# Input and output stored by feature, the first norm applied to projection results, and a different attention tail

## The reference

```
h = rms_norm(x, norm_pre[layer])                 # over the 2048 features of a token
qkv_a, z_a, b_a, g_a, q_b, k_b, v_b, z_b = split(h @ w_in)
qkv_a = silu(causal_depthwise_conv(qkv_a, conv_w))       # 4 taps along the tokens
y_a = rms_norm(gated_delta_rule(...), a_norm) * silu(z_a)
p = softmax(q k^T masked by chunks of 64)
o_b = (p[0] - lam * p[1]) @ v                     # per head, 512 x 128
y_b = rms_norm(o_b, b_norm) * (1 - lam_init) * silu(z_b)
x = x + rms_norm(concat(y_a, y_b) @ w_out, norm_post[layer])
```

## Time and profile before

| | us |
|---|---|
| median of 3 runs | 2717.47 (2712.59 to 2721.62) |
| the profiled execution, its own time | 2727.59 |
| its span, first to last instruction | 2725.3 |
| PE busy | 2550.4 (94% of the span) |
| DVE busy | 1260.8 (46%) |
| ACT busy | 843.0 (31%) |
| POOL busy | 282.2 (10%) |

### The profile page before, as it was taken

How to read it: one execution, slowest core, us unless ns; L and a number is a source line. 1 busy time by engine, 2 the same in 40 slices (tenths; PEclk the granted TensorE clock), 3 DMA queues, 4 the chain that set the end, 5 groups by cost and what they waited for, 6 DMA issues and landing times.

```text
span 2725.3 us, 31273 instructions
## 1 busy us (share of the span) xinstructions
PE 2550.4 (94%) x12516; PEld 2114.8 (78%) x12516; DVE 1260.8 (46%) x1642; ACT 843.0 (31%) x1320; POOL 282.2 (10%) x190
## 2 busy tenths in 40 slices
PE   5999999999999998899978979999999999998897
PEld 4788787888877777888866758888888888887666
DVE  4554545554454447562255455334433344334644
ACT  4232323232244344442232341222212222223333
POOL 0010010202100100001140150000000000013104
PEclk9999999999999999999989989999999999998898
DMA  8932322165344331452212212333333332222211
GB/s 183 106 71 52 63 49 69 39 63 56 70 113 80 75 84 64 130 177 96 100 55 70 70 51 89 96 97 95 97 93 91 100 100 92 101 93 70 70 62 70
DMA packets 221721, 231.84 MB, mean 85 GB/s; under 512 B 9392, under 2 KB 214448, under 8 KB 220848
## 3 DMA queue, kind: packets, MB, share of 16 engines
q1 hardware_dynamic: 221472, 229.83, 33.8%
q10 hardware_dynamic: 144, 0.52, 0.1%
HBM read 221.94 MB, written 8.39 MB: 85 GB/s over the span
## 4 chain that ended last, share of the span: by engine, by line
PE 62%; issue 22%; DVE 7%; POOL 5%; ACT 3%; DMA 1%; DVEq 0%; SPq 0%; POOLq 0%; ACTq 0%
PE acc L757 19%; PE acc L759 18%; PE acc L758 18%; POOL residual L1731 3%; POOL work L1684 2%; DVE weights_lo L1107 1%; ACT weights_hi L365 1%; PE m L912 1%; PE m L1010 1%; PE m L736 1%; DVE work L1505 1%; ACT work L675 1%; PE m L920 1%; DMA work<-in_lambda 1%; PE m L1036 1%
## 5 line engine op out<-in xcount | busy, mean ns | idle before, releaser
L757 PE MATMUL acc<-input_hi,weights_hi 128*128 128x512 f32 (+1 forms) x3200 | 1268.8, 397 | 75.6 <-DVE input_lo L1499 42.4
L759 PE MATMUL acc<-input_hi,weights_lo 128*128 128x512 f32 (+1 forms) x3200 | 1234.8, 386 | 0.0
L758 PE MATMUL acc<-input_lo,weights_hi 128*128 128x512 f32 (+1 forms) x3200 | 1234.4, 386 | 0.0
L1107 DVE TENSOR_TENSOR weights_lo<-weights_raw,weights_hi 128x1024 fp32r<-128x1024 f32 x400 | 497.2, 1243 | 962.1 <-ACT weights_hi L365 961.6
L757 PEld LDWEIGHTS acc<-input_hi,weights_hi 128*128 128x128 f32 x3200 | 613.0, 192 | 216.4 <-issue 67.0
L365 ACT ACTIVATE weights_hi<-weights_raw 128x1024 fp32r<-128x1024 f32 x400 | 423.2, 1058 | 1026.9 <-PE acc L759 1004.9
L759 PEld LDWEIGHTS acc<-input_hi,weights_lo 128*128 128x128 f32 x3200 | 611.4, 191 | 121.8
L758 PEld LDWEIGHTS acc<-input_lo,weights_hi 128*128 128x128 f32 x3200 | 613.2, 192 | 111.2 <-issue 1.9
L1723 POOL TENSOR_TENSOR work<-work 128x512 f32<-128x512 f32 x56 | 72.3, 1291 | 1145.5 <-ACT work L629 1141.1
L1667 POOL TENSOR_TENSOR small<-small 128x4 f32<-128x4 f32 (+1 forms) x20 | 25.8, 1289 | 817.2 <-DVE small L1295 429.7
L1731 POOL TENSOR_TENSOR residual<-residual,work 128x512 f32<-128x512 f32 x59 | 93.0, 1609 | 43.7 <-DVE work L1505 43.7
(11 more groups left out here) (235 smaller groups left out, 1812.6 us busy)
## 6 DMA issues: line engine op xcount, KB each, us to landing
weights_raw<-in_ab_w_in SPq DMA_DIRECT2D x128, 512.0 KB, 5.2
weights_raw<-in_c_w_in SPq DMA_DIRECT2D x128, 512.0 KB, 3.7
weights_raw<-in_m_w_kv SPq DMA_DIRECT2D x32, 512.0 KB, 3.4
weights_raw<-in_ab_w_out SPq DMA_DIRECT2D x32, 512.0 KB, 3.2
weights_raw<-in_m_w_q SPq DMA_DIRECT2D x32, 512.0 KB, 3.3
weights_raw<-in_c_w_out SPq DMA_DIRECT2D x32, 512.0 KB, 3.2
weights_raw<-in_m_w_o SPq DMA_DIRECT2D x16, 512.0 KB, 3.2
work<-in_x SPq DMA_DIRECT2D x4, 1024.0 KB, 10.8
```

The lines of the kernel that those rows point to most:

```text
L757: pe.matmul(out, w_hi[:, o:o + P], hi(kt), start=kt == 0, stop=False)
L758: pe.matmul(out, w_hi[:, o:o + P], lo(kt), start=False, stop=False)
L759: last = pe.matmul(out, w_lo[:, o:o + P], hi(kt), start=False, stop=kt == last_kt)
L1107: TTO(w_lo[:, s * CW:(s + 1) * CW], raw[:, c * CW:(c + 1) * CW], w_hi[:, s * CW:(s + 1) * CW].bitcast(F32), ALU.subtract).then_inc(lo_read ...
```

## The change

Five edits. (1) The host passes x transposed, [16, 128, 512], so `residual` is loaded directly; ACT makes the high part of x times gain, DVE the low part (a scalar_tensor_tensor), and the spill buffer goes: the read-back takes x again. (2) The inverse root mean square is left out of the projection's input and applied when layer 0's projections are evacuated (`take_z`, `convolve`, `keep`, the gate columns). Squares of x are made by ACT, summed by POOL over the 16 tiles, by PE over partitions. (3) The first two column groups, z and q, alternate: chunk order z0 q0 z1 q1 and so on for 8 chunks, with x tiles between the loads; the gate columns move behind chunk 7. (4) Attention's last product swaps its operands, so the output stands by token; ACT's square gives each token's sum at once; DVE scales, PE turns the tile by 4 transposes (hop `ft`), and the hops get weights of their own. (5) The output is stored by feature straight from `residual`, and one more of the last adds goes to DVE.

```diff
@@ hops
-    B_HOPS += ["fs" + _h, "fb" + _h]
+    B_HOPS += ["ft" + _h]
-VECTOR_ADDS = (1, 4, 7, 10, 13)
+B_REPLY = {"vt": 1.2, "a": 0.8, "a00": 2.0, "a10": 2.0, "b": 1.2, "b03": 1.8, "b13": 1.8, "f": 0.6}
+D_SLOTS, B_SLOTS = weighted(D_HOPS, 12, 63, D_REPLY), weighted(B_HOPS, 18, 63, B_REPLY)
+VECTOR_ADDS = (1, 4, 7, 10, 13, 15)
+START_SPLITS = {(0, 0): 0, (0, 1): 1, (1, 1): 2, (1, 3): 3, (2, 1): 4, (2, 3): 5, (3, 1): 6, (3, 3): 7}
+def start_chunk(c):
+    return (c % 2, 4 * (c // 2)) if c < 8 else (c // 4, 4 * (c % 4))
@@ ACT, start
-            for k in range(KT):
-                act.wait_ge(*SM(f"tr{k}"))
-                act.activation(xt(k), start_banks[k % 4], ACT.Copy).then_inc(*SA.did(f"copy{k}"))
-                if k:
-                    start_high(k - 1)
+            def start_high(k):
+                act.wait_ge(x_in[k], 16)
+                act.activation(H_hi[:, k * T:(k + 1) * T], xt(k), ACT.Copy, scale=pcol("norm_pre", k))\
+                    .then_inc(*SA.did(f"hi{k}"))
+            for q in range(4):
+                for n in range(4):
+                    start_high(4 * q + n)
+                    if (q, n) in START_SPLITS:
+                        split(C_AB + START_SPLITS[q, n])
+                for n in range(4):
+                    start_square(4 * q + n)
@@ PE, gates (now at c == 8)
+                        if k == 2:
+                            pe.wait_ge(*SG("sum"))
+                            for t in range(TT):
+                                last = pe.matmul(M[0][:, t:t + 1], sq_sum[:, t * P:(t + 1) * P], ones, ...)
+                        if k == 14:
+                            pe.wait_ge(*SG("pow"))
+                            rows(lambda t: M[2][:, t * P:(t + 1) * P], lambda t: powed[:, t:t + 1], TT)
@@ attention tail: ACT, PE, DVE
-                    act.activation(o_sb, M[3], ACT.Copy).then_inc(*BA.did())
-                    act.activation(o_sq, M[3], ACT.Square).then_inc(*BA.did(f"o{name[1]}"))
+                    for t in range(TT):
+                        act.activation(o_sq[:, o], M[3][:, o], ACT.Square, accum_out=stat[:, t:t + 1])
-                        last = pe.matmul(M[0][:, t:t + 1], o_sq[:, t * P:(t + 1) * P], ones, start=True, stop=True)
-                else:
-                    last = rows(lambda t: M[0][:, t * P:(t + 1) * P], lambda t: powed[:, t:t + 1], TT)
+                else:
+                    pe.wait_ge(*BV("on" + name[2], i))
+                    for t in range(TT):
+                        last = pe.transpose(M[0][:, t * P:(t + 1) * P], o_sb[:, t * P:(t + 1) * P], ident)
+                elif name in ("b03", "b13"):
+                    dve.wait_ge(*BA("o" + h, i))
+                    TS(stat[:, 0:4], stat[:, 0:4], 1.0 / HD, EPS, ALU.mult, ALU.add).then_inc(*BV.did("stat" + h))
+                    dve.wait_ge(*BG("pow" + h, i))
+                    TTO(tiles(o_sb), tiles(M[3]), over_row(powed[:, 0:4], TT, P), ALU.mult).then_inc(*BV.did("on" + h))
-                    then(STT(out=o_sb, in0=o_sb, scalar=b_gain, in1=M[0], op0=ALU.mult, op1=ALU.mult))
-                    TTO(y, y, o_sb, ALU.mult).then_inc(*BV.did(f"y{h}"))
+                    STT(out=y, in0=M[0], scalar=b_gain, in1=y, op0=ALU.mult, op1=ALU.mult).then_inc(*BV.did(f"y{h}"))
@@ DVE, evacuation of layer 0
+                TTO(conv_in, bank(1 + sec, n), rs[:, :], ALU.mult).then_inc(acc_free, 1)
-                TS(dst, src, tap(3), None, ALU.mult).then_inc(*EV.did())
+                TS(dst, conv_in, tap(3), None, ALU.mult).then_inc(*EV.did())
-                dve.tensor_copy((qc, kc, vc)[sec][:, n * T:(n + 1) * T], bank(1 + sec, n)).then_inc(acc_free, 1)
+                TTO((qc, kc, vc)[sec][:, n * T:(n + 1) * T], bank(1 + sec, n), rs[:, :], ALU.mult).then_inc(acc_free, 1)
+            def take_z(it, like):
+                dve.wait_ge(chunk_used, 7 if like == 0 else ab_done(P_AB + 4 * it))
+                for n in range(2):
+                    TTO(xt(z_head(it, like, n)), bank(0, n), rs[:, :], ALU.mult).then_inc(acc_free, 1)
@@ end
-            for n in range(16):
-                act.wait_ge(*FM(f"o{n}"))
-                act.activation(yt(n), acc[n % 4][:, :], ACT.Copy).then_inc(*FA.did(f"o{n}"))
-                for j in range(4):
-                    last = pe.transpose(acc[n % 4][:, j * P:(j + 1) * P], ...)
+            for k in range(KT):
+                sp.wait_ge(*(FV if k in VECTOR_ADDS else FG)(f"x{k}"))
+                sp.dma_start(dram["out"][k], xt(k)).then_inc(out_done, 16)
```

More of the change, by code:

```diff
@@ L269, in build @@
         VA, VV = steps("conv_act"), steps("conv_vec")
-        FM, FA, FV, FG = (steps("final_" + n) for n in ("mm", "act", "vec", "pool"))
+        TA, TV = steps("z_act"), steps("z_vec")
+        FV, FG = steps("final_vec"), steps("final_pool")
         block = ctx.enter_context(nc.Block())
@@ L310, in ab_loads, with start_loads, x_tiles, both @@
                     load_pair(dram["ab_w_in"], col + sec, C_AB + 16 * like + 4 * j, n)
-                    if like == 0 and j == 0:
-                        for k in range(KT):
-                            sp.wait_ge(*SA(f"copy{k}"))
-                            sp.dma_start(dram["spill"][k], xt(k)).then_inc(spilled, 16)
+            def start_loads():
+                def x_tiles(first, end):
+                    for k in range(first, end):
+                        sp.dma_start(xt(k), dram["x"][k]).then_inc(x_in[k], 16)
+                def both(q):
+                    for j, sec in enumerate((3072, 0)):
+                        load(dram["ab_w_in"], sec, C_AB + 2 * q + j, 4 * q)
+                x_tiles(0, 2)
+                load(dram["ab_w_in"], 3072, C_AB, 0)
+                x_tiles(2, 4)
+                load(dram["ab_w_in"], 0, C_AB + 1, 0)
+                x_tiles(4, 8)
+                both(1)
+                x_tiles(8, 12)
+                both(2)
+                x_tiles(12, KT)
+                sp.dma_start(gate_w.rearrange("p (k n) -> p k n", n=16),
+                             dram["ab_w_in"].rearrange("(k p) n -> p k n", p=P)[:, :, 4096:4096 + 16])\
+                    .then_inc(gate_in, 16)
+                sp.dma_start(const[:, :], dram["constants"][:, 0:RESIDENT_W]).then_inc(consts_in, 16)
+                sp.dma_start(lam_in, dram["lambda"]).then_inc(gate_in, 16)
+                both(3)
+            start_loads()
             ab_loads(0)
@@ L1134, in _ @@
-            for k in range(KT):
-                dve.wait_ge(*SA(f"copy{k}"))
-                dve.wait_ge(*SV.last())
-                STT(out=norm_buf[:, (k % 2) * T:(k % 2 + 1) * T], in0=start_banks[k % 4], scalar=pcol("norm_pre", k),
-                    in1=rs[:, :], op0=ALU.mult, op1=ALU.mult).then_inc(*SV.did(f"norm{k}"))
-                if k:
-                    start_low(k - 1)
-                    split_ahead(split, k - 1, C_AB)
-            start_low(KT - 1)
+            split(C_AB + 8)
@@ L1671, in _ @@
             pool.wait_ge(const_set, 2)
+            for k in range(1, KT):
+                pool.wait_ge(*SA(f"sq{k}"))
+                if k > 1:
+                    pool.wait_ge(*SG.last())
+                pool.tensor_tensor(sq_sum, sq_sum if k > 1 else sq_in[:, 0:T], sq_in[:, k * T:(k + 1) * T], ALU.add)\
+                    .then_inc(*SG.did("sum"))
             pool.wait_ge(*SV("stat"))
```

232 lines of the change are left out of this document (96 added, 136 removed).

## The result

| | before | after |
|---|---|---|
| median of 12 runs, us (lowest to highest) | 2717.35 (2712.59 to 2724.55) | 2704.56 (2698.85 to 2711.59) |
| ratio after / before | | 0.995, 95% interval 0.994 to 0.996 |
| profiled execution, span | 2725.3 | 2700.1 |
| a second profiled execution, span | 2715.7 | 2697.1 |

What follows compares the result with a forecast made beforehand. PE was taken as the bound, busy 94% of the span. Start -8.3, attention -4.8, end -3.2 and evacuation +3.6 sum to -12.7 us, from the median of 2717.5 to 2705; range 2687 to 2719.

Steps and rivals of the forecast that it cites:

- The start: Stretch up to chunk 8: PE would start chunk 8 at 89.3 us, a gain of 8.3 us.
- four chunks at 5.9 (23.6) and four at 6.4 (25.6): Start: load times in us of the first eight weight chunks, at 89 and 82 GB/s, before chunk 7 has landed.
- rival B: Start: first loads no longer slow, PE bound by itself, chunk 8 at 71, total 2689 us; chance 0.18.
- The 2 us allowed for the gate columns: Start: estimated extra load time for the small pieces of the gate columns.
- a third through, 1.2 a round: Evacuation in delta rounds: of 3.6 us more DVE work a round, PE feels 1.2; +3.6 us for three rounds.
- My upper bound of +11: Evacuation in delta rounds: the highest cost allowed for the added DVE work, in us, beside the booked +3.6.
- my -9.9: Attention tail: four transposes replace 16 small matmuls in PE's queue, -1.24 us for each of eight heads.
- 2 for each of the two heads: Memory projections: PE waits 2 us per head for DVE's delayed split; with 0.6 for squares and 1.5 ending round 7, +5.1.
- Rival D: Attention tail: DVE's stand at `b03` and `b13` holds the split in every round, +32 us, total 2732; chance 0.10.
- The end: Last adds and stores: tile 15 on DVE, span ends at 2722.1 instead of 2725.3, -3.2 us.
- C: Delta rounds: DVE taps with two SBUF inputs contend with POOL, +5 us seen by PE, total 2710; chance 0.14.
- E: Start: loads take 6.7 us each and x comes slower in 2 KB pieces; gain only 1.5, total 2712; chance 0.10.

Runs made afterwards that it cites:

- in_order: Changed kernel with its first eight weight chunks loaded in the order of before (z's four, then q's four): 2727.96 us, 1.003 of before.
- no_scale: Changed kernel without the inverse-root scaling of the delta heads' q, k and v, taps reading the projection's bank as before: 2695.99 us, 0.9911 of before.
- spread_taps: Changed kernel with q's and k's three later taps spread over a chunk's slots in rounds 1 to 3, ACT's tanh a chunk later: 2684.09 us, 0.9855 of before.
- after_pad: Changed kernel with 112 more instructions that only wait at the head of PE's program: 2704.79 us.

## Why the prediction was right, and where it was wrong

**The sum was right by cancellation.** The start gave 11 us more than its term and rounds 1 to 4 cost 6 to 12 more than theirs. That these met was luck.

**Start, wrong step: "four chunks at 5.9 (23.6) and four at 6.4 (25.6)".** I took the price of a load from windows in which one column group is read to its end, and laid it on an order that changes group with each load. in_order gives just that price back, 47.5 for my 49.2; alternated it is 32.7. So PE, not the loads, set the pace from 20 us on, which was rival B's mechanism (chunk 8 at 71; measured 77.8), while B's reason, that the loads' slowness belongs to the spill or to start traffic, is false: in_order has no spill and slow loads. The edit that I had passed over as a reordering is worth 23 us, more than the whole gain. The 2 us allowed for the gate columns had no row behind them: that transfer landed 0.9 us behind the one ahead.

**Evacuation, mis-sized: "a third through, 1.2 a round".** About half passed: 5.6 us of waits for 12 of DVE work, in four rounds and not three. Two terms were missing: z in chunk 5 (+3.1, booked as hidden) and the stops at the loop's restart (+2.5 in the first pair, +4.6 in the second). My upper bound of +11 was near what happened. That DVE's added work ahead of its answers costs PE is shown by no_scale; that its length in one piece matters, by spread_taps, with ACT's share unparted. What z costs is read from the rows alone; no run takes it out.

**Attention: the saving right, the cost wrong.** Four transposes take 0.35 (793.74 to 794.09):

```profile
793.74 0.60 PE L942 MATMUL m<-constants,work 128*128 128x128 f32 x4
794.09 0.47 PE L785 MATMUL acc<-input_hi,weights_hi 128*128 128x512 f32 x1
```

From chunk 80 to 160, without PE's idle time and with half of each us at the low clock, PE's work fell by 10.5 us in both pairs, for my -9.9. The wrong step is "2 for each of the two heads", +5.1 in all: PE's idle time in that stretch went from 23.2 to 24.4, +1.2. PE waits for splits in the memory projections for 6.5 us before and 6.6 after, so DVE's stand at `b03` and `b13` is covered there too. At the end of round 7, where 1.5 was forecast, PE waited 3.49 for DVE before; now 3.43 and 1.00, in two places. Rival D is out: in rounds 5 to 7 PE waits once for a split, 0.7 us. Together that is -9.3; it shows as -6.9 and -6.3 because after has 5 us more of PE's work at the low clock, 2.4 by the estimate, in the first pair and 6 in the second.

**The end, right**: 9.3 us from DVE's last norm steps to the end of the span before, 5.25 after, -4.0 for -3.2. The other 1.9 of that stage lie in and behind the last chunk, ahead of the first norm step, and go with the clock: in both profiles of after only 2 us of PE's work in this stage were at the low clock. In after_pad they were 7, and its stage takes 39.35, 3.5 under before.

**C** is out as a cost to PE. Contention is there, but for three taps that meet POOL, which take 2.61 for 0.75, not for two thirds of them at half as much again; and PE's waits don't fall when it is taken away. **E** is out: the loads are cheaper, and x tiles in pieces of 2 KB land 0.6 to 0.7 us apart, some 400 GB/s.

## What to carry to other kernels

Take the price of a transfer from rows with the same neighbours in the queue; an edit that only permutes loads can be worth more than those that remove work. Where an engine answers another in small steps, cut its long blocks (here four dependent operations, 4 us) into pieces that stand between the answers, before counting how much work they hold: that, with ACT's step moved a chunk later, gave 20.7 us for no operation fewer, the scaling itself cost 8.8. Look at single operations behind a mean: 1030 ns was 0.75 us for most and 2.61 for three. And a forecast that meets the total proves nothing until its terms are compared stage by stage.

## What the runs showed of the hardware

- Loads of 512 rows by 1 KB from ab_w_in cost 47.5 us for eight, one column group after the other, and 32.7 and 33.1 alternating between two groups, with the DMA engines at a share of 1.00 or more in the window of 20 to 35 us of all three.
- PE's code came in 16 KB packets, and a loop of rounds 1 to 3 was fetched anew in none, one or both of its further iterations, with stops of PE of 0 to 6.6 us in all; the same program (before) did it once and not at all in two executions.
- A tap on DVE with two SBUF inputs took 2.61 us where it met a multiply of POOL (three of 20) and 0.75 elsewhere; with one input in PSUM it took 0.75 beside the same multiply.
